# Masked groups first in a recurrence, roundings on ScalarE and a spread convolution in a two-block kernel

## The reference, cut to what matters

```
def gated_delta_chunked(q, k, v, beta, g, s0):        # 8 heads of 128
    lmat = where(strict, (kb @ k.T) * decay, 0)
    tmat = inverse(eye + lmat)
    u, wk = tmat @ (v * beta), tmat @ (kb * exp(g))
    def step(state, inp):
        v_new = u_i - wk_i @ state
        o_i = q_i @ state + attn_i @ v_new
        state = state * exp(gl_i) + k_i.T @ v_new

def rwkv7_scan(r, w, k, v, kk, b_vec, s0):             # 16 heads of 64, two to a pair
    def step(state, inp):
        sa = -state @ kk_t
        state = state * w_t + outer(sa, b_t) + outer(v_t, k_t)
        out = state @ r_t
```

```
proj = h @ w_in; q, k, v, g_attn, glu_a, glu_b, g_conv = split(proj)
y_attn = softmax_with_sink(q k.T / 8 + bias) v * silu(g_attn)
u = glu_a * sigmoid(glu_b); u = conv31(u) + conv_b
y_conv = (silu(layer_norm(u)) @ w_pw + b_pw) * silu(g_conv)
x = layer_norm(alpha * x + gate * (concat(y_attn, y_conv) @ w_out))
```

## Time and profile before

| | |
|---|---|
| runs | 3923.34, 3928.7 and 3930.75 us, median 3928.7 |
| profiled execution | 3914.84 us |
| span of its instructions | 3913.0 us |
| mean TensorE clock granted | 0.944 of full speed |
| TensorE busy in the span | 3410.2 us (87%) |
| VectorE busy | 2264.5 us (58%) |
| ScalarE busy | 1036.2 us (26%) |
| GpSimd busy | 909.0 us (23%) |

### The profile page before, as it was taken

One profiled execution on the slowest core, in us unless ns is written; L12 is line 12 of the kernel. 1 busy time (PEld: TensorE's weight loads), 2 busy tenths in 40 slices (PEclk: granted clock), 3 DMA queues, 4 the chain that ended last, 5 costly groups with the idle time before them and its releaser, 6 DMA issues. The chain is left out here.

```text
span 3913.0 us, 50830 instructions
## 1 busy us (share of the span) xinstructions
PE 3410.2 (87%) x19656; PEld 2844.0 (73%) x19656; DVE 2264.5 (58%) x4083; ACT 1036.2 (26%) x1712; POOL 909.0 (23%) x707
## 2 busy tenths in 40 slices
PE   8679999989999588888888868887997988889897
PEld 1168888868888488788888867885776766677485
DVE  2544565655555467777767746775103789996323
ACT  1214555543333112122212212222002221221202
POOL 0000000000000112122212200000675665656174
PEclk9889999999999799999999969998998999999998
DMA  9122343445455445455545433322523221212232
GB/s 383 44 74 93 125 140 124 140 127 179 154 176 183 106 99 135 115 130 132 131 115 131 124 95 108 129 88 84 198 86 113 75 70 61 74 59 81 79 115 75
DMA packets 337340, 464.70 MB, mean 119 GB/s; under 512 B 189856, under 2 KB 236032, under 8 KB 330608
## 3 DMA queue, kind: packets, MB, share of 16 engines
q1 hardware_dynamic: 272576, 364.28, 30.0%
q0 software_dynamic: 26512, 83.08, 7.1%
q10 hardware_dynamic: 38048, 14.56, 1.6%
HBM read 382.80 MB, written 81.63 MB: 119 GB/s over the span
## 5 line engine op out<-in xcount | busy, mean ns | idle before, releaser
L988 POOL TENSOR_TENSOR w_high<-ring_o,cst 128x1024 fp32r<-128x1024 f32 x152 | 304.3, 2002 | 427.9 <-PE pjl L1009 276.8
L990 POOL TENSOR_TENSOR w_low<-ring_o,w_high 128x1024 fp32r<-128x1024 f32 x152 | 386.8, 2545 | 11.9
L1007 PE MATMUL pjl<-high,w_high 128*128 128x512 f32 x816 | 332.0, 407 | 29.0 <-DVE low L2562 15.6
L2953 DVE SCALAR_TENSOR_TENSOR arena<-arena,par 128x512 f32<-128x512 f32 x232 | 323.2, 1393 | 7.4
L1008 PE MATMUL pjl<-low,w_high 128*128 128x512 f32 x816 | 324.5, 398 | 0.0
L1009 PE MATMUL pjl<-high,w_low 128*128 128x512 f32 x816 | 323.3, 396 | 0.0
L1992 POOL DMA_DIRECT2D arena_r<-in_w_ada x256 | 138.0, 542 | 719.1 <-DVE arena_r L2341 661.0
L1981 POOL MEMSET unused<- 128x1 f32 x3 | 0.2, 98 | 1102.3 <-POOLq L197 1102.3
L1139 DVE TENSOR_TENSOR wl_in<-ring,wh_in 128x1024 fp32r<-128x1024 f32 x136 | 164.2, 1221 | 133.5 <-ACT wh_in L1132 133.4
L1120 PE MATMUL pjl<-h_high,wh_in 128*128 128x512 f32 x544 | 214.4, 394 | 9.1 <-DVE wl_in L1139 9.1
L1120 PE MATMUL xu<-h_high,wh_in 128*128 128x512 f32 x544 | 220.6, 405 | 0.0
(11 more groups left out here) (474 smaller groups left out, 8018.8 us busy)
## 6 DMA issues: line engine op xcount, KB each, us to landing
ring<-in_w_lr SPq DMA_DIRECT2D x136, 512.0 KB, 4.2
arena_r<-in_w_ada POOLq DMA_DIRECT2D x256, 256.0 KB, 3.2
arena<-in_w_ada SPq DMA_DIRECT2D x32, 1024.0 KB, 11.5
ring_o<-in_w_out SPq DMA_DIRECT2D x64, 512.0 KB, 3.7
ring_o<-in_w SPq DMA_DIRECT2D x64, 512.0 KB, 3.4
arena_r<-rk_d SPq DMA_DIRECT2D x94, 192.0 KB, 4.7
rk_d<-arena_p SPq DMA_DIRECT2D x72, 192.0 KB, 1.9
arena_p<-gate_rows SPq DMA_DIRECT2D x32, 386.0 KB, 6.1
```

Of the source, the lines that this page charges most:

```text
L988: pool.tensor_tensor(h, w, one, ALU.mult).then_inc(S[done + "h"], 1)
L990: pool.tensor_tensor(l, w, h.bitcast(F32), ALU.subtract).then_inc(w_used, 1)
L1007: pe.matmul(lat, wh[:, c], ah, start=kk == 0, stop=False)
L2953: link(dve.scalar_tensor_tensor(ca[:], x[:, o:o + LAT], w[:, o:o + 1], ca[:], ALU.mult, ALU.add))
```

## The change

Three parts.

In the recurrence the groups are ordered LC, MB, MC, BT, CT, CV. Slots 1 and 2 hold the two LC, slots 3 and 4 two MB and two MC, 5 to 8 BT and CT, 9 both CV. The 15 block steps go 4, 3, 4, 4 over slots 5 to 8, `inverse_turn` is in slot 8, ScalarE's half of the loads in slot 10. The multiply-adds of `later` go to slots 0, 2, 8, 9, 11, 13 (two), 14 (two), 15, 16 (three) and 17 (three). SyncE's loads of the next operands wait on the transposes' count instead of the products'.

In the delta recurrence values and keys are turned in slots 15 and 16 instead of 13 and 14.

In phase two's loop the rounding of the 64 halves moves from GpSimd to ScalarE (`rounded`, `ahead`), interleaved with its other work, and GpSimd only subtracts; `heads(1)` moves behind the last tile's evacuation; and the convolution's steps are divided otherwise around the attention's parts. The gate tiles and the output product are split on GpSimd as before.

```diff
-G_VALUES, G_KEYS = 13, 14
+G_VALUES, G_KEYS = 15, 16
...
-LATER = {0: 1, 1: 1, 2: 2, 3: 1, 4: 1, 11: 1, 12: 1, 13: 2, 14: 1, 15: 2, 16: 2, 17: 1}
-R_GROUPS = {n: range(n - 1, n) for n in range(1, 9)} | {9: range(8, 10), 10: range(10, 12)}
-R_STEPS = {5: range(0, 5), 6: range(5, 10), 7: range(10, 15)}
-R_TURNED, R_DONE, R_BACK = 5, 7, 9
+LATER = {0: 1, 2: 1, 8: 1, 9: 1, 11: 1, 13: 2, 14: 2, 15: 1, 16: 3, 17: 3}
+R_GROUPS = {1: (0,), 2: (1,), 3: (2, 3), 4: (4, 5), 5: (6,), 6: (7,), 7: (8,), 8: (9,), 9: (10, 11), 10: ()}
+R_STEPS = {5: range(0, 4), 6: range(4, 7), 7: range(7, 11), 8: range(11, 15)}
+R_TURNED, R_DONE, R_BACK = 5, 8, 10
...
-    GROUPS = [(name, d) for name in ("BT", "CT", "LC", "MB", "MC", "CV") for d in range(2)]
+    GROUPS = [(name, d) for name in ("LC", "MB", "MC", "BT", "CT", "CV") for d in range(2)]
...
-                sp.wait_ge(S["r_q"], i * 16 + 14)
+                sp.wait_ge(S["r_p"], i * 12 + 12)
...
-            split_weights(pool, e, "n_done", loads(half), 0, A + 4 * BODY + 16 + EARLY)
+            pool.memset(unused[:, 9:10], 0.0).then_inc(S["n_doneh"], 4 * BODY)
+            with pool.Fori(0, BODY) as i:
+                for s in range(RING):
+                    pool.wait_ge(S["n_hi"], i * RING + s + 1)
+                    pool.tensor_tensor(e["parts"][1][:, s % 2], ring[:, s].rearrange("p k c -> p (k c)"), e["parts"][0][:, s % 2].bitcast(F32),
+                                       ALU.subtract).then_inc(w_used, 1)
+
+            split_weights(pool, e, "n_done", loads(half_g), 4 * BODY, 16 + EARLY)
...
+            for n in range(2):
+                act.wait_ge(w_loaded[n], loads(half) + 16)
+                act.activation(e["parts"][0][:, n], ring[:, n].rearrange("p k c -> p (k c)"), ACT.Copy).then_inc(S["n_hi"], 1)
...
+            def rounded(n):
+
+                act.wait_ge(w_loaded[n % RING], loads(half) + 16 + n // RING * 16)
+                if n >= 2:
+                    act.wait_ge(S["n_done"], DONE + n - 1)
+                act.activation(e["parts"][0][:, n % 2], ring[:, n % RING].rearrange("p k c -> p (k c)"), ACT.Copy).then_inc(S["n_hi"], 1)
+
+            def ahead(t, which):
+
+                if 2 * t + 2 + which < 4 * BODY:
+                    rounded(2 * t + 2 + which)
...
+                T = 8 * i
+                ahead(T, 0)
                 act.wait_ge(S["n_done"], hw + 2)
                 act.activation(qs[:, 0], P0, ACT.Copy).then_inc(S["n_ev"], 1)
+                ahead(T, 1)
+                ahead(T + 1, 0)
                 act.wait_ge(S["n_done"], hw + 4)
                 act.activation(qs[:, 1], P0, ACT.Copy).then_inc(S["n_ev"], 1)
+                ahead(T + 1, 1)
                 soft(0)
+                ahead(T + 2, 0)
...
                 flip(3)
-                heads(1)
+                ahead(T + 7, 0)
                 act.wait_ge(S["n_done"], hw + 16)
                 act.wait_ge(S["n_y"], 1 + i * 2 + 1)
                 act.activation(ga[:], P0, ACT.Copy)
                 act.activation(gs[:], P0, ACT.Sigmoid).then_inc(S["n_ev"], 1)
+                ahead(T + 7, 1)
+                heads(1)
...
+                before(0, 4)
                 if i:
-                    conv(u - 1, 0, 4)
                     gate(i - 1, 1)
-                    conv(u - 1, 4, 12)
+                before(4, 20)
                 rows(i, 0)
+                before(20, 22)
                 norm(i, 0)
-                if i:
-                    conv(u - 1, 12, 22)
+                before(22, 24)
                 rows(i, 1)
+                before(24, 26)
                 norm(i, 1)
-                if i:
-                    conv(u - 1, 22, 31)
+                before(26, 31)
                 unit(u)
-                conv(u, 0, 12)
+                conv(u, 0, 9)
                 rows(i, 2)
+                conv(u, 9, 11)
                 norm(i, 2)
-                conv(u, 12, 16)
+                conv(u, 11, 13)
                 rows(i, 3)
+                conv(u, 13, 15)
                 norm(i, 3)
                 unit(u + 1)
-                conv(u, 16, 22)
+                conv(u, 15, 20)
                 gate(i, 0)
-                conv(u, 22, 31)
+                conv(u, 20, 31)
```

More of the change, by code:

```diff
@@ L2025, in _ @@
             blocks_back(0)
-            sp.wait_ge(S["r_q"], 6)
+            sp.wait_ge(S["r_p"], 6)
             load_a(0, 1)
@@ L2035, in _ @@
                 blocks_back(i * 2 + 2)
-                sp.wait_ge(S["r_q"], i * 16 + 22)
+                sp.wait_ge(S["r_p"], i * 12 + 18)
                 load_a(i + 1, 1)
@@ L2058, in group @@
                     pe.wait_ge(S["r_pa"], a * 2 + 2)
-                elif n < 6:
-                    pe.wait_ge(S["r_pe"], a * 4 + n - 1)
+                elif n < 8:
+                    pe.wait_ge(S["r_pd"], a * 8 + n - 1)
                 else:
-                    pe.wait_ge(S["r_pd"], a * 8 + n - 5)
+                    pe.wait_ge(S["r_pe"], a * 4 + n - 7)
                 if name == "MB" and d == 0:
@@ L2192, in group @@
                 if name in ("BT", "CT"):
-                    act.wait_ge(S["r_p"], a * 6 + 2 + n + 1)
+                    act.wait_ge(S["r_p"], a * 6 + 2 + n - 6 + 1)
                     act.activation((BT[hh] if name == "BT" else CT)[:, d], tp[:, d], ACT.Copy).then_inc(S["r_pe"], 1)
@@ L2289, in group @@
                     return
-                dve.wait_ge(S["r_q"], a * 8 + n - 4 + 1)
+                dve.wait_ge(S["r_q"], a * 8 + (n if n < 6 else n - 4) + 1)
                 if name == "CV":
@@ L2840, in _ @@
                 act.activation(ab[:], P0, ACT.Copy).then_inc(S["n_ev"], 1)
+                ahead(T + 2, 1)
                 flip(0)
                 soft(1)
+                ahead(T + 3, 0)
                 act.wait_ge(S["n_done"], hw + 8)
                 act.activation(sb_[:], P0, ACT.Sigmoid).then_inc(S["n_ev"], 1)
+                ahead(T + 3, 1)
                 flip(1)
+                ahead(T + 4, 0)
                 act.wait_ge(S["n_done"], hw + 10)
@@ L2848, in _ @@
                 act.activation(ab[:], P0, ACT.Copy).then_inc(S["n_ev"], 1)
+                ahead(T + 4, 1)
                 heads(0)
                 soft(2)
+                ahead(T + 5, 0)
                 act.wait_ge(S["n_done"], hw + 12)
                 act.activation(sb_[:], P0, ACT.Sigmoid).then_inc(S["n_ev"], 1)
+                ahead(T + 5, 1)
                 flip(2)
                 soft(3)
+                ahead(T + 6, 0)
                 act.wait_ge(S["n_done"], hw + 14)
@@ L2858, in _ @@
                 act.activation(gs[:], P0, ACT.Sigmoid).then_inc(S["n_ev"], 1)
+                ahead(T + 6, 1)
                 flip(3)
-                heads(1)
+                ahead(T + 7, 0)
                 act.wait_ge(S["n_done"], hw + 16)
@@ L2964, in _, with before @@
                 u = 2 * i
+                def before(a, b):
+                    if i:
+                        conv(u - 1, a, b)
+                before(0, 4)
                 if i:
-                    conv(u - 1, 0, 4)
                     gate(i - 1, 1)
-                    conv(u - 1, 4, 12)
+                before(4, 20)
                 rows(i, 0)
+                before(20, 22)
                 norm(i, 0)
-                if i:
-                    conv(u - 1, 12, 22)
+                before(22, 24)
                 rows(i, 1)
+                before(24, 26)
                 norm(i, 1)
-                if i:
-                    conv(u - 1, 22, 31)
+                before(26, 31)
                 unit(u)
-                conv(u, 0, 12)
+                conv(u, 0, 9)
                 rows(i, 2)
+                conv(u, 9, 11)
                 norm(i, 2)
-                conv(u, 12, 16)
+                conv(u, 11, 13)
                 rows(i, 3)
+                conv(u, 13, 15)
                 norm(i, 3)
                 unit(u + 1)
-                conv(u, 16, 22)
+                conv(u, 15, 20)
                 gate(i, 0)
-                conv(u, 22, 31)
+                conv(u, 20, 31)
             conv(7, 0, 4)
@@ L3068 @@
 o_y0 o_y1 o_y2 o_y3 o_y4 o_y5 o_y6 o_y7 o_w o_x o_xx o_r o_ss o_sq o_v o_rt o_n o_h o_b o_bd o_bm o_done o_doneh o_yh o_yl o_hh o_hl
-n_done n_doneh n_vt n_ysh n_ysl n_xa n_xs n_pw n_kv n_dup n_ev n_at n_sc n_p n_tr n_pt n_pv n_y n_ks n_cv n_m n_x n_u n_v0 n_v
+n_done n_doneh n_hi n_vt n_ysh n_ysl n_xa n_xs n_pw n_kv n_dup n_ev n_at n_sc n_p n_tr n_pt n_pv n_y n_ks n_cv n_m n_x n_u n_v0 n_v
 z_g z_gm z_xs z_s z_sq z_ss z_u z_y z_r z_c z_rt z_n z_i z_m z_rr z_o z_st""".split()
```

## The result

| | before | changed |
|---|---|---|
| median of the runs | 3927.7 us | 3905.2 us |
| ratio | | 0.994, 95% interval 0.9924 to 0.9955 |
| profiled execution, span | 3914.8, 3913.0 us | 3900.5, 3898.8 us |

The changed kernel is 22.5 us faster. The median of the kernel before is of four executions here, one more than ahead of the prediction.

What follows compares the result with a forecast made beforehand. VectorE bounds phase two's loop; in the recurrence TensorE and VectorE hand work to and fro. Terms -67 - 6 + 18 - 10 = -65, less 4 for unforeseen waits: -61, so 3854 profiled, 3868 median; range 3828 to 3908.

Steps and rivals of the forecast that it cites:

- Loop of phase two, -67: Phase two's loop: roundings moved to ScalarE relieve VectorE, 500 to 433 us, 67 less; bounds 35 and 78 less.
- Rival B: Phase two's loop: VectorE stays the bound, 118 us in three groups, only 30 us less; 3907 us, chance 0.10.
- D: Phase two's loop: ScalarE's queue makes tiles late, costing 61 to 122 us, kernel near 3990; chance 0.08.
- Gate tiles, -6: Behind phase two's loop: first gate tile's convolution begins 3 us behind TensorE, not 9; 6 us less, bounds 0 and 10.
- Delta scans, -10: Delta scans: turning values and keys in slots 15 and 16 saves 1.4 us in each of seven scans, 10 less.
- The recurrence, +18: Recurrence of `phase_rwkv`: new order of groups, block steps and `later` cost 18 us; bounds -20 and +40.
- 7 x 0.1 + 7 x 2.8 = 20 us: Recurrence, serial VectorE count: even scans 57.3 against 57.2, odd ones 58.4 against 55.6; 20 us more.
- the late set: Recurrence, slot 3: MB needs GpSimd's loaded set before it lands; odd scans stall 2.8 us, even ones 1.1.
- step 4: Recurrence, serial count: step 4 starts at 36.0 in even scans (landing 33.5), at 34.1 in odd ones (31.7).
- 1.5 us in each scan: Recurrence: clock falls in the new stalls, 1.5 us in each scan, named within the upper bound of +40.
- rival A: Recurrence: the 80 us of waits on L2361 and L2353 halve, 20 us shorter; 3830 us, chance 0.12.
- Rival C: Recurrence: new load wait and clock are paid in every scan, +40 us; 3890 us, chance 0.08.

Runs made afterwards that it cites:

- order only: Kernel before with only the new order of groups and their waits, block steps and `LATER` as before: 3929.7 us, ratio 1.0004.
- + new steps: Kernel before with the changed recurrence (group order and block steps), but `LATER` as before: 3948.7 us, ratio 1.0051.
- + new `LATER`: Kernel before with the changed recurrence (group order and `LATER`), but block steps as before: 3972.5 us, ratio 1.0118.

## Why the prediction was right in sign and wrong in size

**Loop of phase two, -67: right.** It gave 72: 67 in the last three groups, 5 in the first and its start. The group takes 106.0 us (forecast 108, and 107 for the first), the start costs 1.9 us more as forecast (the first wait for ScalarE is 6.4 us instead of 4.5). The step's mean was put near 1.1 us and is 1.015. Clock 1.00. Rival B (VectorE stays the bound) and D (ScalarE late) did not occur: TensorE waits for neither norm nor a subtraction. A change of ScalarE's table takes 1.28 us, and an activation that is ready follows at once:

```profile
3159.77 1.28 ACT L2894 ACT_TABLE_LOAD   x1
3161.06 0.60 ACT L2894 ACTIVATE arena<-pjl 128x512 f32<-128x512 f32 x1
```

The 2.66 us of the Trainium skill (ScalarE: Activation LUTs, What ACT_TABLE_LOAD costs), of which 1.38 are a drain, are not seen here. What the Trainium skill says (GPSIMD Engine Reference, Key points: shared SBUF interfaces with VectorE) agrees as far as that a step beside a subtraction is still held (up to 2.96 us for 0.75). The estimate from it was 131 us given back to VectorE, the rows' 77. VectorE's busy time fell by 91 us (2264.5 to 2173.3), 71 of them (to 2193.9) with the roundings alone, so one held instruction for each rounding was the better price; the other 20 came with the new division.

**Gate tiles, -6: wrong, and covered.** VectorE's first step on the last channel was expected 3 instead of 9 us behind TensorE. It starts 8.5 us after TensorE's first gate tile (3501.3 and 3492.8), against 8.8 before (3514.8 and 3506.0), and the wait stayed 9.2. VectorE is done with `gate(3, 0)` 8.9 us ahead of that tile instead of 3.3, but the new division puts 11 steps instead of 9 behind it, which take 17.4 us instead of 12.1. What follows the loop is 1 us shorter, not 6; the loop's groups gave the rest.

**Delta scans, -10: right** (-9.7 in the two spans, -11.6 alone), and L712's wait for L915 went as forecast.

**The recurrence, +18: here it failed.** The failing step is "7 x 0.1 + 7 x 2.8 = 20 us", the serial count of even and odd scans. Measured from one scan's first L2126 to the next one's, even scans take 60.3 us against a forecast of 57.3 and odd ones 62.9 against 58.4. Against the kernel before (57.0 and 57.4) the two terms are 3.3 and 5.5. The 2.8 was counted from 55.6, an odd scan at full clock, while the new length had to be set against the mean, 57.4: by its own count an odd scan would have lost 1.0. Of the small terms, scan 0 lost 2.6 instead of gaining 1, the prologue gained 0.6 instead of 3.5, which can't be told from nothing, and the last scan's `later` steps cost 2.3 behind the last L2126, forecast 2.5. In that count

- the late set was right: odd scans wait 19.2/7 = 2.7 us, forecast 2.8 (even ones do not wait, forecast 1.1);
- the pair's start was right: L2402 costs 31.0 - 11.4 = 19.6 us over seven, 2.8 each, forecast 2.55;
- the turn in even scans was right (over at 28.2, forecast 27.9; landing 34.0, forecast 33.5). In the odd scans of the middle (5, 7 and 9) the turn was over at 27.2 to 27.7 and the landing came at 33.9 to 34.2, forecast 26.1 and 31.7: the way itself took 6.5 to 6.7 us instead of 5.7. VectorE stands 3.2 us a scan for the blocks, forecast up to 2.5;
- step 4 was set 2.5 us behind the landing. It left out L2085, the twelve matmuls that stand on TensorE between L2313 and L2126. In the odd scan above, whose blocks land as L2313 starts at 1960.28, L2126 starts at 1963.91, 3.6 us later;
- the clock was left at full in the sum. "1.5 us in each scan" stood in the text as the upper bound. The busy time says 22.6 us, 1.5 in each of 15 scans: the bound was the value. It is part of why the first step of even scans, behind the memset's wait, takes 9.6 us (1867.15 to 1876.72), forecast 7.6.

The gain of rival A's kind was there (37 us off the two old waits) and was more than paid for. Rival C, +40 and 3890, had the nearest mechanism, and was itself 27 us short in the recurrence. Rival B's 3907 is the nearest time, by chance, for the loop did not do what B says. That the median fell inside the range is luck of the same kind: the range took in B's slower loop and no such recurrence.

The runs part the 60 us of the recurrence alone: order of groups 1, block steps 25 (19.5 with the new `LATER`), `LATER`'s last two slots 34 to 39, slots 8 and 9 nothing. By the medians, 63 us in all, it is 3, 18 and 42, so the block steps are the smaller of the two costs by either and their sizes are known to some 8 us. Why the order alone helps odd scans and slows even ones by as much was not tried: even scans alone carry the last pair's output work on VectorE ahead of the turn, which is an argument, not a run.

## What to carry to other kernels

Measure the parts of a mixed change alone: here a loss of 63 us hid in a gain of 91, and the kernel without it is 68 us faster than the one that was made. Where a scan is bound by handovers, work that nobody waits for must not stand at the end of the scan on the queue that starts the next one: 0.85 us of it cost about its own length in every scan ahead of the state, and more where it also released a transfer. In a serial count write down every engine between a landing and the next start, set the result against the mean and not the best scan, and where TensorE will stall as long as here (3.9 and 4.4 us) count the matmuls behind it at half clock.

## What the runs showed of the hardware

Waiting cost more clock where it stood in one place. By the trace's records of the granted clock, the recurrence of "order only" has 64.9 us at half clock with 109.8 us of waits; that of "+ new steps" has 99.0 with 123.5, 53.2 of them in front of one line. "+ new `LATER`", with its waits in more places, has 85.3 with 144.2. In the changed kernel 119.5 us are at half clock, in the kernel before 54.6; the recurrence of before has 47.8 to 68.3 in its five executions. This is read from few executions and was not tested by itself.

The blocks' way through DRAM is 1.1 us longer (6.7 for 5.6) in odd scans when two slices of `w_ada` are released beside it. In scan 6 of the changed kernel, where one slice is in flight beside the way and the second is issued only as the last loads are under way, it takes 6.0.

A step of the convolution is still held for up to 2.96 us under GpSimd, but the 16 scalings of the probabilities are not held once (1224 to 1227 ns), where the earlier trace rows has a median of 3203.
